# Expert gather by halves, and a separate wait for each half of its copy, in a mixture-of-experts inference step

## The reference, cut to what matters

```
for e in range(N_EXPERTS):                      # 32 experts
    hid = silu(xt @ w1[e]) * (xt @ w3[e])       # xt: 320 tokens x 1024; w1, w3: 1024 x 256
    y = y + combine[:, e:e+1] * (hid @ w2[e])   # w2: 256 x 1024
```

## Time and profile before

| | |
|---|---|
| median of three runs | 898.04 us |
| the profiled execution's own time | 901.33 us |
| its span in the trace | 899.5 us |
| mean granted TensorE clock | 0.919 |
| TensorE matmul busy | 773.7 us (86%) |
| VectorE, ScalarE, GpSimd busy | 374.6, 185.2, 149.4 us |
| DMA | 220.27 MB, mean 245 GB/s |

### The profile page before, as it was taken

One profiled execution on the slowest core, in us unless ns is written; L12 is line 12 of the kernel. 1 busy time (PEld: TensorE's weight loads), 2 busy tenths in 40 slices (PEclk: granted clock), 3 DMA queues, 4 the chain that ended last, 5 costly groups with the idle time before them and its releaser, 6 DMA issues. The chain is left out here.

```text
span 899.5 us, 20897 instructions
## 1 busy us (share of the span) xinstructions
PE 773.7 (86%) x8753; PEld 461.1 (51%) x8753; DVE 374.6 (42%) x687; ACT 185.2 (21%) x426; POOL 149.4 (17%) x300
## 2 busy tenths in 40 slices
PE   5999899989779899968886787989869997799985
PEld 2445466656566666743554565546654444444421
DVE  2130533229842245556872776624262222422213
ACT  2012122116341111012421321223111110111112
POOL 8400030007040020022042333331000000000000
PEclk9999899988988959968899899999869998999998
DMA  8622141212320302438899999986919999999993
GB/s 311 273 93 117 47 156 47 88 55 86 121 48 16 112 9 57 99 106 327 279 395 415 422 373 423 418 329 265 372 57 386 422 425 421 424 422 425 421 424 109
DMA packets 53240, 220.27 MB, mean 245 GB/s; under 512 B 21872, under 2 KB 24219, under 8 KB 28827
## 3 DMA queue, kind: packets, MB, share of 16 engines
q1 hardware_dynamic: 45456, 184.66, 53.1%
q0 software_dynamic: 7040, 34.10, 9.7%
q10 hardware_dynamic: 650, 0.18, 0.1%
HBM read 211.82 MB, written 7.09 MB: 243 GB/s over the span
## 5 line engine op out<-in xcount | busy, mean ns | idle before, releaser
L230 PE MATMUL bank<-arena 128*128 128x320 f32 x256 | 83.9, 472 | 3.7 <-PEq L112 3.7
L208 POOL DMA_DIRECT2D arena<-in_cv x112 | 59.1, 528 | 127.5 <-PE bank L1885 95.5
L546 PE MATMUL bank<-arena 128*128 128x336 f32 x224 | 71.3, 474 | 4.2 <-DVE arena L712 4.2
L2574 DVE TENSOR_TENSOR arena<-arena,bank 128x512 f32<-128x512 f32 x40 | 27.5, 688 | 108.2 <-PE bank L2362 105.2
L1522 DVE STREAM_TRANSPOSE arena<-arena 128x2048 f32<-128x2048 f32 x28 | 63.1, 2288 | 11.4 <-DMA arena<-in_ck 10.2
L2385 PE MATMUL bank<-arena 128*32 128x512 f32 x512 | 63.3, 596 | 3.5 <-DMA arena<-in_w_exp 2.8
L511 PE MATMUL bank<-arena 128*128 128x512 f32 (+1 forms) x144 | 65.0, 610 | 1.5 <-DMA arena<-in_w_zb 1.5
L230 PEld LDWEIGHTS bank<-arena 128*128 128x128 f32 x256 | 49.1, 202 | 25.3 <-issue 9.4
L546 PEld LDWEIGHTS bank<-arena 128*128 128x128 f32 x224 | 43.9, 200 | 27.4 <-issue 10.0
L1885 PE MATMUL bank<-arena 128*16 128x128 f32 x1024 | 32.9, 289 | 21.9 <-issue 18.7
L1340 ACT ACTIVATE arena<-bank 128x384 f32<-128x384 f32 (+6 forms) x63 | 25.9, 443 | 122.6 <-PE bank L230 46.2
(11 more groups left out here) (476 smaller groups left out, 1105.7 us busy)
## 6 DMA issues: line engine op xcount, KB each, us to landing
arena<-in_w_exp SPq DMA_DIRECT2D x99, 1024.0 KB, 19.9
arena<-in_ck SPq DMA_DIRECT2D x120, 256.0 KB, 6.1
arena<-in_cv POOLq DMA_DIRECT2D x112, 256.0 KB, 7.1
arena<-in_w_gate SPq DMA_DIRECT2D x8, 1024.0 KB, 4.8
arena<-in_w_za SPq DMA_DIRECT2D x7, 1024.0 KB, 6.9
arena<-in_w_zb SPq DMA_DIRECT2D x6, 1024.0 KB, 16.0
arena<-in_cv SPq DMA_DIRECT2D x16, 256.0 KB, 3.6
arena<-in_w_proj SPq DMA_DIRECT2D x8, 512.0 KB, 11.4
```

The lines of the kernel that those rows point to most:

```text
L208: eng.dma_start(tile[n:P:4, :], src[bass.ds(page, 1)].rearrange("a (p j) n -> (a p) (j n)", j=4))\
L230: mm = nc.tensor.matmul(bank[b][:, 0:TM], w[:, k, a, :], xnT[:, k, NMETA:T], start=(k == 0), stop=(k == KT - 1))
L546: mm = nc.tensor.matmul(bank[j % 2][:, 0:T], w[:, k, (j % 2) * P:(j % 2 + 1) * P], xnT[:, k, :], start=(k == 0), stop=(k == KT - 1))
```

## The change

In `gather`, the 4 UP matmuls are issued, then the 8 matmuls of the first half, then the 4 DN matmuls, then the 8 of the second half. Before, the 8 UP and DN matmuls came first, in turn. No matmul is added or dropped. In `hidden`, part 0 waits for the copy of the first half alone, and part 1 waits for the copy of the second.

```
 def gather(dst, lhs_sel, name):
-    for k in range(4):
-        for half, r in enumerate((UP, DN)):
+    for half, r in enumerate((UP, DN)):
+        for k in range(4):
             nc.tensor.matmul(bank[half][:, k * P:(k + 1) * P], x2[r, NHT - 1, k * P:(k + 1) * P],
                              lhs_sel[r, NT - 1, :], start=(k == 0), stop=False)
-    for half in range(2):
         for k in range(4):
             for i in range(NT - 1):
                 mm = nc.tensor.matmul(bank[half][:, k * P:(k + 1) * P], ...
         mm.then_inc(S(name), 1)
...
 def hidden(q, part):
+    pe.wait_ge(S("xg_sb"), 2 * q + part + 1)
     if part == 0:
-        pe.wait_ge(S("xg_sb"), 2 * q + 2)
         if q:
             pe.wait_ge(S("hid_ready"), q)
```

## The result

The changed kernel is slower: 908.63 us median of six runs (904.55 to 917.32) against 899.47 for the kernel before in the same session (six runs, 895.63 to 903.33). The ratio is 1.0098, with a 95% interval of 1.0063 to 1.0133. The forecast was 898.6 us in a range of 895.6 to 902.3. A ratio leaves out executions that took over 1.5% more than the fastest of their kernel: none of these twelve, but a few further down, the profiled one of e14 among them.

What follows compares the result with a forecast made beforehand. The prediction took the weight loads to bound the kernel. The first gather's 1.29 us less 0.69 us of wait starts them 0.60 us later, which on the 898.04 us median gives 898.6 us, range 895.6 to 902.3.

Steps and rivals of the forecast that it cites:

- The loads are the bound: Expert stage: loads run without a gap from the first issue to the last weights; a later start moves the end one for one.
- A gather at full clock: Each gather: 1.09 us for the separate DN group plus 0.20 us for two added shape changes, 1.29 us longer.
- The 64-row group of one half: In each gather: four matmuls of one half take 8 steps, 1.09 us, what 8 pairs took.
- The waits of quad 3 for loads: TensorE in quad 3: its 2.42 us of waiting for loads vanish under a delay of 4.47 us.
- the sum: TensorE's delays less its waits for loads: overflow pass starts 2.05 us later, with loads starting 0.60 us later.
- The last load still ends last: Quad 7: TensorE comes 8.50 us late against 10.59 us of waits, leaving 2.1 us; the tail is unchanged.
- SyncE's queue: After the overflow pass: issues start 3.3 us later, at 783.8, 5.6 us before the queue would run dry.
- The margin: After the overflow pass: the load issued last landed near 789.4, so issues at 783.8 come 5.6 us in time.
- The clock in the pass: Overflow pass: its gather adds 1.29 us, though it is at half clock in its first part.
- The first gather: Quad 0: 1.29 us longer less 0.69 us of wait, so loads start 0.60 us later; bounds -0.7 to +1.9.
- TensorE becomes the bound, in quad 7: Rival, chance 0.17: gathers grow by more than 1.55 us, outputs(7) starts after the last load; 902.9 us at the upper bound.
- The gather's price is hidden: Rival, chance 0.10: in the gathers, DN matmuls overlap the 128-row ones and hidden(0, 0) starts early; 897.4 us.
- A starved queue: Case of a loss over 1%, chance 0.03 together with a gather some 2.5 us longer; sign: DMA rate gap after 783 us.

Runs made afterwards that it cites:

- e14: Changed kernel with the old gather order in quad 0 alone; ratio 1.0016 to the kernel before.
- e4: Kernel before with the new wait and quad 0's first hidden products run between the two halves of its gather; ratio 1.0009 to the kernel before.
- e1: Kernel before with the new wait alone, old gather order; ratio 0.9996 to the kernel before.
- e6: Kernel before with the new gather order in quads 5 to 7 alone, old wait; ratio 1.0005 to the kernel before.
- e7: Kernel before without the overflow pass, old gather and wait; ratio 0.9891 to the kernel before, median 892.92 us.
- e9: Kernel before with seven more products in the overflow pass alone; ratio 1.0036 to the kernel before.
- e10: Kernel before with three more products in the overflow pass alone; ratio 1.0006 to the kernel before.
- e2: Kernel before with the new gather order alone, old wait; ratio 1.0105 to the kernel before.
- e5: Kernel before with the new gather order in quads 0 to 4 and the overflow pass, old wait; ratio 1.0073 to the kernel before.
- e8: Changed kernel without the overflow pass; ratio 0.9941 to the kernel before, median 895.87 us.
- e11: Changed kernel with the old gather order in the overflow pass alone; ratio 1.0056 to the kernel before.
- e12: Changed kernel with four of the overflow pass's eight hidden products left out, its rows wrong; ratio 1.0056 to the kernel before.
- e13: Kernel before with the new gather order in quad 0 alone and the new wait; ratio 1.0023 to the kernel before.
- e3: Kernel before with four more 64-row matmuls ahead of each of the nine gathers, old order and wait; ratio 1.0116 to the kernel before.

## Why the prediction was wrong

**Right.** The loads are the bound, and the train moves with its start: from a first issue 9.4 to 12.0 us after the stage's start (e4, before) it is 205.8 to 206.3 us long in all six kernels with the pass and without a deep gap. A gather at full clock is 1.27 us longer (680.51 to 686.68 against 678.44 to 683.34 on the chain), with 1.29 forecast. The 64-row group of one half takes what the pairs took: 680.44 to 681.53 is 1.09 us. Narrow windows of after at the change of shape in the gather of quad 1:

```profile
683.30 0.28 PE L2352 MATMUL bank<-arena 128*128 128x128 f32 x1
683.51 0.37 PE L2348 MATMUL bank<-arena 64*128 64x128 f32 x1
```

The 64-row record starts 0.07 us ahead of the end of the 128-row one, as at the change in the other direction. The Trainium skill, TensorEngine Tiling (Array Packing), section Key Properties, speaks of a drain at such a change; the trace shows a step of 0.21 us in place of 0.11, and by its modelled ends no full drain.

The waits of quad 3 for loads vanish (3.64 us at 746.61). At the overflow pass TensorE is 1.42 us later against the first issue (78.77 in place of 77.35; the sum gave 2.05 - 0.60 = 1.45). The last load still ends last, after 2.21 us of waiting, with 2.1 forecast; that match is partly luck, as the loads and TensorE were both later than in the sum.

**The step that failed is "SyncE's queue"**, which ended in "The DMA does not starve". It failed in three terms.

1. *The wrong release.* I held 3.3 us of lateness against the first issue after the pass, and stopped there. That issue lets only three loads go, 7.4 us of transfer; the next ones wait for quad 3's outputs, behind another gather, and went out at 790.25 before. I never did the subtraction for them, and it is the tighter place.
2. *The margin.* I took it from the landing of the last load issued, and read that too late: the row of 763 to 765 belongs to an issue that had begun at 761.22, so the load landed at 787.6 and not at 789.4. But no landing says how much is still to be moved. Bytes do. Before, from the first issue to each of the two releases:

```profile
675.07:780.48 105.41, 92.74 (x604) 42.73 (x596) 25.54 (x49) 14.23 (x29) 0.00 (x0) 0.97 1.00 417
675.07:790.25 115.18, 101.59 (x687) 48.62 (x680) 30.36 (x60) 16.29 (x33) 0.00 (x0) 0.97 1.00 417
```

At 780.48, 44 loads had been issued since 675.07, 46.14 MB at 1.0486 MB each, and 105.41 us at 417 GB/s had moved 43.96. So 2.2 MB were left, 5.1 us at 425 GB/s, where my reading gave 8.9 (789.4 - 780.48). At 790.25 it is 47 loads, 49.28 MB less 48.03: 1.25 MB, 2.9 us. The table has 2.2, as the rate needs a moment after an issue (156 GB/s in 676 to 677, 377 in the next us). In after the same count leaves 0.1 MB at the first release and nothing at the second:

```profile
677.14:787.78 110.64, 98.33 (x604) 48.00 (x596) 25.51 (x49) 14.22 (x29) 0.00 (x0) 0.94 1.00 416
677.14:798.80 121.66, 108.42 (x687) 54.90 (x680) 30.36 (x60) 16.29 (x33) 0.00 (x0) 0.94 0.98 406
```

Even my own sum, 1.45 + 1.29 + 1.29 = 4.0 us of lateness at outputs(3), is beyond this margin, by 1.8 us.

3. *The clock in the pass.* I priced its gather at 1.29 us, as if the DN group met full clock. From the start of the pass to its hidden products it took 10.24 us in place of 8.09, so 2.15 more: counted from the pass's start, the granted clock was 0.50 in the first 4 us in both kernels, and in the next 4 us 0.62 in place of 0.86. The eight records of line 2450 took 5.40 us in place of 3.70, with 0.68 granted in place of 1.00; that these 1.70 us come from the change is not shown (last section). The first 8 us of the pass in before, then the same in after and its line 2450:

```profile
752.42:756.42 4.00, 4.00 (x25) 3.78 (x26) 0.17 (x1) 0.00 (x0) 0.00 (x0) 0.50 1.01 414
756.42:760.42 4.00, 3.66 (x28) 3.42 (x26) 0.00 (x0) 1.23 (x3) 0.00 (x0) 0.86 1.01 420
```

```profile
755.91:759.91 4.00, 4.00 (x17) 3.78 (x18) 0.17 (x1) 0.00 (x0) 0.00 (x0) 0.50 1.02 426
759.91:763.91 4.00, 4.00 (x22) 3.65 (x21) 0.00 (x0) 0.60 (x1) 0.00 (x0) 0.62 1.02 424
775.60:781.00 5.40, 5.39 (x8) 2.00 (x8) 0.00 (x0) 0.60 (x1) 0.00 (x0) 0.68 1.00 422
```

Together: 1.42 + 2.15 + 1.70 + 1.24 (the gather of quad 4) = 6.5 us of lateness at outputs(3), the 122.0 - 115.5 of the table. Less the margin of 2.2 it is 4.3; the train grew by 4.4.

**The first gather** was sized at +0.60 us, with a bound of +1.9. The first issue came 0.82 later in the pair of profiles. Over the profiles of kernels with the old order there and no padding (before, e1, e6, e7, e9, e10, e14) it lies 10.4 to 12.1 us after the stage's start, with the new order (after, e2, e5, e8, e11, e12, e13) 12.0 to 15.6. The two longest, e2 and e11, are those whose second 64-row group ran at half clock throughout, 2.00 us for 8 records in e2's chain:

```profile
666.69 2.00 PE bank L2350 x8
668.70 3.39 PE bank L2355 x16
```

The five of these with the order and wait of before average 11.6 us, the five with the order and wait of the change 12.9: 1.3 us later, about halfway between the value chosen and the bound.

**Rivals.** *TensorE becomes the bound, in quad 7* had the right sign and the wrong place: the 2.21 us of waiting left and the trains of e5 and e6 show that quad 7's slack holds. Its own price, 902.9 us, lay outside the range that was said to hold it. *The gather's price is hidden* fell by the 1.27 us. A starved queue stood in the text with a gap in the rate after 783 us as its sign, which is what came, but only in the 0.03 of cases past 1%.

**Open.** The train and the first gather make 4.4 + 0.8 us in the profiles. The medians differ by 9.2 us, with an interval from 5.7 to 12. e12, whose train is only 0.7 us longer, is still at 1.0056, and e14, with a long train, at 1.0016. So nearly half of the loss has no cause shown.

The runs on record give one lead. Within one kernel, time goes with the mean granted clock of the run: some 6.3 us less for each 0.01 more. This is an estimate, from one line fitted through all 243 runs that the ratios use and that have a clock, with a level for each kernel. The changed kernel's runs average 0.911, those of the kernel before 0.918. Beside each other, in us against the kernel before: the levels at equal clock (1.3 to 1.9 to each side), and the first issue and the train of the one profile, added up.

| kernel | at equal clock | first issue + train |
|---|---|---|
| changed | 4.4 | 5.2 |
| e2 | 7.4 | 8.2 |
| e3 | 3.7 | 3.7 |
| e5 | 5.1 | 5.4 |
| e9 | 2.7 | 2.9 |
| e11 | 2.6 | 4.9 |
| e12 | 1.5 | 1.1 |
| e14 | 1.9 | 2.0 |
| e13 | 1.1 | -0.2 |
| e10 | 0.5 | 0.0 |
| e6 | -0.3 | -1.2 |
| e4 | -1.6 | -2.8 |
| e1 | -2.2 | -1.0 |

All but e11 agree within 1.4 us. So what the train and the first gather leave over of the changed kernel's time went with a lower granted clock in its runs. Whether the new order lowers the clock, and where, is not shown: no run was made for it.

## What to carry to other kernels

When the loads are the bound, list what the issuing queue waits for, in order, around the longest stretch in which nothing is freed, and subtract the lateness at every release and not at the first one alone. Each release lets out only so many loads. Count what is in flight as bytes issued less bytes moved; the landing of the last load, read rightly, said 7.1 us here (787.6 - 780.48) where bytes said 5.1. Two matmuls of 64 rows on opposite halves of the array ran for the price of one here, so an order that parts them costs what it parts. An engine with 86% busy and slack at its end can have almost none in the middle.

## What the runs showed of the hardware

- Half-height matmuls of 128 columns: 8 records of one half take 1.09 us, and so do 16 records that alternate between the halves.
- The granted clock falls or rises at different moments in executions of like kernels. The eight records of the pass's output products took 3.70 us in the profiles of six kernels with the pass, and 5.36 to 5.40 in eight, two of them with the old order in that pass and ahead of it from quad 1 on (e6, e13). So the 1.70 us of term 3 are not shown to come from the change. The 26 records behind the last load took 3.62 us in eleven of the sixteen profiles, and 4.94 to 6.44 in five (e1, e3, e4, e8, e9).
- The stage began at 657.9 to 668.0 us from profile to profile, with the code ahead of it unchanged: more than any effect studied here.
